# Latent scores issued after the turning of the near probabilities in each attention step of a one-core trunk step

## What is computed

```python
# 8 neighbourhood heads: window keys with bias + all context keys, one softmax
s_all = concat([s_loc + bias (masked outside the window), s_ctx])
o_na  = softmax(s_all) @ concat([v_window, v_ctx])
# 4 differential heads, two maps each, over all context and all latent keys
p    = softmax(q[m] @ concat([ck, k])[m].T * d**-0.5)      # m = 0, 1
o_df = (p[0] - lam * p[1]) @ concat([cv, v])
```

## Time and profile before

| What | Value |
|---|---|
| time of the three runs | 1995.19 us median, 1993.63 to 1995.66 |
| time of the profiled execution | 1993.7 us |
| its span | 1991.9 us |
| mean granted clock of TensorE | 0.982 |
| TensorE busy (matmul) | 1929.0 us, 97% of the span |
| VectorE busy | 1655.7 us, 83% |
| ScalarE busy | 1384.5 us, 70% |
| HBM traffic | 318 GB/s over the span |
| attention stage | about 216 to 470 us of the span |
| expert stage | about 470 us to the end |

### The profile page before, as it was taken

How to read it: one execution, slowest core, us unless ns; L and a number is a source line. 1 busy time by engine, 2 the same in 40 slices (tenths; PEclk the granted TensorE clock), 3 DMA queues, 4 the chain that set the end, 5 groups by cost and what they waited for, 6 DMA issues and landing times.

```text
span 1991.9 us, 25173 instructions
## 1 busy us (share of the span) xinstructions
PE 1929.0 (97%) x9620; PEld 1333.1 (67%) x9620; DVE 1655.7 (83%) x1636; ACT 1384.5 (70%) x1625; POOL 187.8 (9%) x99
## 2 busy tenths in 40 slices
PE   9999889975999999999999999999999999999998
PEld 8999667653666666666666666666666666666665
DVE  3777566667898989898989898888989898989897
ACT  3222456645777787878787878787787878787876
POOL 0000212122010101010110101010101010110100
PEclk9999799987999999999999999999999999999999
DMA  9543501156999999999999999999999999999994
GB/s 384 201 175 154 184 27 57 50 180 223 386 358 397 382 387 379 369 384 369 396 357 398 352 404 351 403 355 384 379 380 377 370 391 362 397 363 394 350 390 179
DMA packets 102934, 636.33 MB, mean 319 GB/s; under 512 B 11584, under 2 KB 21824, under 8 KB 30112
## 3 DMA queue, kind: packets, MB, share of 16 engines
q1 hardware_dynamic: 97696, 618.19, 79.6%
q0 software_dynamic: 4832, 16.50, 3.0%
q10 hardware_dynamic: 288, 0.03, 0.0%
HBM read 620.02 MB, written 13.88 MB: 318 GB/s over the span
## 4 chain that ended last, share of the span: by engine, by line
PE 75%; ACT 1%; DVE 0%; issue 0%; DVEq 0%
PE ps L1566 16%; PE ps L1565 16%; PE ps L1570 16%; PE ps L1582 8%; PE ps L1583 8%; PE ps L1587 8%; PE ps L1545 1%; PE ps L1536 0%; ACT place L1675 0%; ACT place L1671 0%; ACT place L1678 0%; DVE place L1730 0%; ACT place L1623 0%; ACT place L1673 0%; DVE place L1746 0%
## 5 line engine op out<-in xcount | busy, mean ns | idle before, releaser
L722 DVE TENSOR_TENSOR place<-ring,place 128x2048 fp32r<-128x2048 f32 x527 | 1224.4, 2335 | 144.6 <-ACT place L718 141.0
L718 ACT ACTIVATE place<-ring 128x2048 fp32r<-128x2048 f32 x528 | 1009.7, 1916 | 310.7 <-PE ps L1570 235.1
L1565 PE MATMUL ps<-place 128*80 128x512 f32 x1408 | 561.1, 399 | 1.8 <-DVE place L1686 1.8
L1566 PE MATMUL ps<-place 128*80 128x512 f32 x1408 | 555.6, 395 | 0.0
L1570 PE MATMUL ps<-place 128*80 128x512 f32 x1408 | 381.4, 392 | 0.0
L1570 PEld LDWEIGHTS ps<-place 128*80 128x80 f32 x1408 | 208.2, 148 | 115.8 <-issue 0.7
L1566 PEld LDWEIGHTS ps<-place 128*80 128x80 f32 x1408 | 209.2, 149 | 107.1 <-issue 0.7
L1565 PEld LDWEIGHTS ps<-place 128*80 128x80 f32 x1408 | 208.6, 148 | 107.5 <-DVE place L1686 2.0
L1582 PE MATMUL ps<-place 128*80 128x512 f32 x704 | 280.5, 398 | 0.0
L1583 PE MATMUL ps<-place 128*80 128x512 f32 x704 | 277.1, 394 | 0.0
L1587 PE MATMUL ps<-place 128*80 128x512 f32 x704 | 190.4, 392 | 0.0
(11 more groups left out here) (210 smaller groups left out, 1766.3 us busy)
## 6 DMA issues: line engine op xcount, KB each, us to landing
ring<-in_w_exp SPq DMA_DIRECT2D x528, 1024.0 KB, 6.8
ring<-in_w_late SPq DMA_DIRECT2D x16, 1024.0 KB, 11.2
ring<-in_w_in SPq DMA_DIRECT2D x12, 1024.0 KB, 6.5
ring<-in_w_ada SPq DMA_DIRECT2D x7, 1024.0 KB, 10.0
ring<-in_w_out SPq DMA_DIRECT2D x4, 1024.0 KB, 6.0
place<-in_near_bias SPq DMA_DIRECT2D x16, 256.0 KB, 3.2
ring<-in_xT SPq DMA_DIRECT2D x4, 640.0 KB, 8.6
place<-in_x SPq DMA_DIRECT2D x5, 512.0 KB, 6.3
```

What stands on the lines that cost most here:

```text
L718: eng.activation(wH[:, n % SPLITS, :], ring[:, slot("exp", n), :], ACT.Copy).then_inc(wh_done, 1)
L722: eng.tensor_tensor(wL[:, n % SPLITS, :], ring[:, slot("exp", n), :], wH[:, n % SPLITS, :].bitcast(F32), ALU.subtract).then_inc(chunk_used, 1)
L1565: eng.matmul(out, xH[:, e % 2, kk, :], w, start=(kk == 0), stop=False)
L1566: eng.matmul(out, xL[:, e % 2, kk, :], w, start=False, stop=False)
```

## The change

The latent scores leave `scores(k)` and become a function of their own, `latent_scores(k)`, that is called after the first two turnings of unit `k-1` and ahead of its near values. In steps 4 to 19 TensorE's order becomes: near scores, turning of near probabilities (two pieces), latent scores, near values. Steps of the context tile have no latent scores and stay as they are. The semaphores, their counts and the programs of all other engines are the same.

```diff
@@ -860,10 +860,13 @@
                     mm.then_inc(s_ready, 1)
-                    if t:
-                        for m, h in enumerate(sides):
-                            mm = eng.matmul(ps[:, 2 * m + 1, :], qdf[h, i, own], kdf[h, i, CTX:TOK], start=True, stop=True)
-                        mm.then_inc(s_ready, 1)
+
+                def latent_scores(u):
+                    t, i = unit(u)
+                    own = slice(t * P, (t + 1) * P)
+                    for m, h in enumerate((slice(0, 64), slice(64, 128))):
+                        mm = eng.matmul(ps[:, 2 * m + 1, :], qdf[h, i, own], kdf[h, i, CTX:TOK], start=True, stop=True)
+                    mm.then_inc(s_ready, 1)
@@ -997,6 +1000,9 @@
                     if 1 <= k <= UNITS:
                         turn_p(k - 1, 0)
                         turn_p(k - 1, 1)
+                    if k < UNITS and unit(k)[0]:
+                        latent_scores(k)
+                    if 1 <= k <= UNITS:
                         weigh_near(k - 1, 0)
```

## The result

The change makes the kernel slower: 2002.27 us median over 7 runs against 1993.63 us over 7 runs of before, a ratio of 1.0041 with a 95% interval of 1.0028 to 1.0053. That is 8.6 us, twice what I took as the least that can be told from no change. The first three runs of before, whose median of 1995.19 us the forecast started from, lay 1.5 us high: 23, 28 and 9 later runs beside the experiments have medians of 1993.61, 1993.15 and 1993.45 us. The profiled execution took 2002.27 us, its span 2000.4 us, against 1993.7 and 1991.9. Whole-kernel sums hardly move: TensorE is busy 7.8 us more, VectorE 2.6 us more.

A forecast was written before the change was run, and what follows sets the result against it. TensorE's instruction stream sets the pace in mid-attention. Losses of 0.4 us in steps 4 to 6 and 2.2 in steps 9, 13 and 17, against 2.2 won in six even steps, gave 1995.6 us, range 1992.0 to 1999.5.

The forecast's parts named there:

- slower: TensorE's clock falls in the longer waits: Rival for steps 5, 9 and 17: new slow stretches at half clock add 4.5 us, giving 2000.1 us; chance 0.10.
- Wait for the copy: TensorE's near values: the 0.47 us wait per step for ScalarE's copy of the turned probabilities goes away.
- Row changes: TensorE, two more changes between 64 and 128 weight rows per step: 0.10 us together, the way back free.
- the six winning steps: Steps 8, 10, 12, 14, 16 and 18, where TensorE sets the pace: 0.37 us won each, 2.2 in all.
- Rival 3: Each row change costs 0.24 us more, eating TensorE's gain: 1998.5 us; chance 0.14 together with another rival.
- Bank in steps 9, 13 and 17: Later latent scores delay VectorE's bank reading and the projection: 0.62 us each, 0.16 more in 13 and 17, 2.2 lost.
- The waits of 2.0 and 3.0 us: Sign of being right: the projection's waits for its bank grow to about these in steps 13 and 17.
- Steps 11, 15 and 19: VectorE is late anyway, with 0.74 us of slack in step 11: nothing gained, nothing lost.
- Steps 4 to 6: TensorE waits for ScalarE's exponentials: step 4 loses 0.58 us, steps 5 and 6 win 0.17, together 0.4 lost.
- The clock: TensorE's slow stretches taken as in the profile before; one new stretch had chance 0.14, two or more 0.10.
- Nothing behind the loop: Routing and expert stage after the attention loop only shift as a whole; the time changes by what the loop changes.

The follow-up runs named there:

- turn_first: Kernel before with the two near turnings ahead of all scores from step 4 on: 1999.32 us, ratio 1.0033.
- the filling: Four spare matmuls at each of six TensorE waits in steps 5, 6, 9, 13, 17: kernel before 1987.50 us, changed kernel 1993.39 us.
- filling and moved reading: Projection's bank read between near and latent maxima, spare matmuls only in steps 5 and 6: old order 1984.44 us, new order 1983.30 us.
- late_bank: Kernel before with the new order of latent scores only in steps 9, 13 and 17: 2000.32 us, ratio 1.0038.
- the reading is moved: VectorE reads the projection's bank between near and latent maxima in odd steps 9 to 19: changed kernel 1988.30 us, kernel before 1987.33 us.
- the kernel with six even steps 0.12 us shorter: Kernel before with the new order only in steps 8, 10, 12, 14, 16 and 18: 1995.98 us, ratio 1.0019.

## Why the prediction was wrong

The forecast was no change, 1995.6 us; measured were 2002.27, outside the range. The step that failed most is one that the sum put at nothing: it counted TensorE's clock as unchanged. It had no term either for the squares that meet GpSimd. Two of its terms were mis-sized besides, the row changes and the bank, by an estimated 2.6 us together, of which steps 4 to 6 gave half a microsecond back. The nearest rival is "slower: TensorE's clock falls in the longer waits", with a chance of 0.10. Its mechanism is in the profile: the mean clock is lower in step 5 (0.64 instead of 0.83), 9 (0.86 instead of 1.00) and 17 (0.78 instead of 0.88), the three steps it named. That its price of 2000.1 came near is in part luck, since it held none of the other misses, and the slow stretch of step 13 went away (1.00 instead of 0.87). Step by step:

- *Wait for the copy.* Right. It is gone in steps 8 to 19, and turn_first shows it worth 0.46 us in step 8 against 0.47 by the rows.
- *Row changes, taken as 0.10 us per step.* They cost 0.35, and this mis-sized the six winning steps: 0.12 us each and 0.75 in all, where 0.37 and 2.2 stood. In the changed kernel the last near pair lasts 286.05 - 285.73 = 0.32 us up to the turnings; before, the latent scores follow it after 280.38 - 280.16 = 0.22 us. This is the 0.10 that I had. Six turnings ahead of a 64-row pair last 0.81 instead of 0.66, and the pair 1.06 instead of 0.96. I had taken the way back from 128 to 64 rows as free because no gap stands there in the timeline. Its price sits in the distance between starts: 0.15 on the turnings ahead of the pair and 0.10 on the pair itself. The rule of the Trainium skill that I set against the row (TensorEngine Tiling (Array Packing), Key Properties: a change of mode drains the engine) fits both directions: 0.12 us net in the step tables against 0.47 for the hidden copy. The 0.11 us that I estimated beside it for the two changes was too small as well. Rival 3, that the changes of rows eat the gain, was right in kind: 0.25 us more than I took.
- *Bank in steps 9, 13 and 17, 0.62 us each and 0.16 more in two.* The mechanism was right, the size too small. L952 starts 6.79 us after the first near score of step 9 instead of 5.93, so 0.86; in step 17 VectorE's reduction starts 3.26 us after it instead of 2.19 (365.42 - 363.23), so 1.07 where 0.78 stood. The forecast wait of 1.8 us in step 9 measured 1.79, but that is luck: it was added up from 0.62 for the bank and 0.37 for TensorE's gain, and these came as 0.86 and 0.12. The waits of 2.0 and 3.0 us forecast for steps 13 and 17 measured 2.86 and 1.90. That is the long square, 1.07 us more than its usual 0.29, which moved from step 17 to step 13 and which the sum left out; the rows of before had it inside the wait of 1.89 us in step 17.
- *Steps 11, 15 and 19, taken as nothing.* Steps 11 and 15 are 0.26 and 0.25 us longer, and the projections of all three now wait 0.36 us. The slack of 0.74 us on VectorE was smaller than the delay of the latent scores, which is 0.32 - 0.22 + 0.81 + 0.10 = 1.01 us and not 0.76.
- *Steps 4 to 6, 0.4 us lost.* No such loss shows where the clock stays up in steps 5 and 6: with the filling, and with filling and moved reading, the new order takes 0.1 us less over the three steps. The 4.3 us in the profile are mostly clock, since late_bank shows 3.9 of them in steps 4 to 7 with the old order there.
- *The clock.* I summed a profile whose slow stretches I took as given, with a chance of 0.10 for two more of them. The filling takes 8.9 us from the changed kernel and 5.7 from the kernel before. So the clock costs both kernels, and the changed one some 3 us more. Nor did it fall by length of wait: after 1.79 us in step 9, not after 2.86 in step 13.
- *Nothing behind the loop.* Right within 1.3 us.

How the 8.6 us divide can be estimated. Some 3 us go with the filling. For the 5.9 that remain, the step tables of the two filled kernels add up to 6.0 from step 4 to step 19. Up to the projection, steps 9 and 13 grew by 1.95 and 1.90 us (in step 9 L953 starts 7.87 us after the first near score instead of 5.92), of which the squares are 1.08 and 0.94, by their lengths over 0.29. What is left of them, step 17 (0.98) and steps 11 and 15 (0.54) make 3.4 us for the bank's chain. A slow stretch behind the projection of step 13 is 1.5. The even steps give 0.7 back, and steps 4 to 7 another 0.1. The forecast had 2.2 us for the bank, 2.2 for the even steps and 0.4 for steps 4 to 6, so these terms account for some 2 us of the miss of 8.2, and clock and squares for the other 6. It is one pair of profiles, and the places of squares and slow stretches differ between executions, so the shares of these two hold to a microsecond or two at best: no kernel ran that fixes the place of GpSimd's work. What is shown by medians is that 7.6 of the 8.6 us go when the reading is moved, and that with the filling added the new order is 1.1 us ahead. What makes the clock fall in one wait and not in another stays open.

## What to carry to other kernels

Before moving work ahead of a result that another engine waits for, follow that engine's fixed order to the next thing *your* engine needs from it: here the hidden wait was worth 0.47 us, the row changes took 0.35 back, and the delay came home through VectorE with 0.9 us and more wherever that engine's next reading was awaited. Where TensorE's clock comes and goes, price a change at several runs' clocks, not at one profile's, and consider spare matmuls in a wait: some 24 of them took 5.7 us off a 1993 us kernel. A release that an engine can give early (here the reading of a bank) belongs ahead of that engine's work whose results are needed later.

## What was not expected of the hardware

Changing between 64-row and 128-row weights twice more per step costs 0.35 us at full clock, of which the return to 64 rows has 0.25 with no idle time in the timeline. A custom VectorE instruction over 128 columns took 1.29 to 1.37 us instead of 0.29 beside a GpSimd instruction of 1.25 to 1.27 us, while a VectorE reduction from PSUM kept its 1.55 us beside one of 2.35. TensorE's clock fell after a wait of 0.89 us in one place and stayed up after one of 2.86 us in another. In the kernel with six even steps 0.12 us shorter, slow stretches stand in steps 6 and 9, whose program was the same as before and which had none.
